# Token-major sums of squares ahead of the experts, and roots spread by a product of ones with a diagonal matrix

## The reference

```python
def rms_norm(x, g):
    xf = x.astype(F32)
    y = xf * lax.rsqrt(jnp.mean(xf * xf, axis=-1, keepdims=True) + EPS)
    return (y * g.astype(F32)).astype(x.dtype)

def modulate(x, g, shift, scale):
    return rms_norm(x, g) * (1.0 + scale) + shift
...
        x = x + g1 * m
        h = modulate(x, norm_ffn_g[l], sh2, sc2)
        x = x + g2 * hierarchical_moe(h, moe_w_group[l], moe_w_expert[l], moe_w_gate[l],
                                      moe_w_up[l], moe_w_down[l])
```

## Time and profile before

| | us |
|---|---|
| median of three runs | 918.23 |
| the three runs | 917.15, 918.23, 920.77 |
| the profiled execution | 921.55 |
| its span in the profile | 919.7 |

### The profile page before, as it was taken

The page is one execution under the profiler, slowest core; times in us unless marked ns, Lnnn a source line. Parts: engine busy times, 40 slices in busy tenths (PEclk is TensorE's granted clock), DMA queues, the critical chain, the costliest instruction groups (busy, mean ns, idle before and its releaser), DMA issues.

```text
span 919.7 us, 13173 instructions
## 1 busy us (share of the span) xinstructions
PE 762.9 (83%) x4683; PEld 428.4 (47%) x4683; DVE 359.8 (39%) x852; ACT 151.4 (16%) x358; POOL 176.0 (19%) x283
## 2 busy tenths in 40 slices
PE   1899977899988999877779876988899988778770
PEld 1544433468545655444445533736555544444430
DVE  0314427752353344333333333556234433333243
ACT  3112144630351110000000002443010000000000
POOL 0000210000003133322233220000233332323220
PEclk9999997999996999999999997995799999999995
DMA  9996630002876899999999997978399999999935
GB/s 351 428 407 278 239 61 0 12 1 109 355 292 222 345 409 416 422 420 421 420 421 423 390 424 291 425 320 306 124 400 390 417 423 424 421 422 422 421 123 205
DMA packets 39383, 294.33 MB, mean 320 GB/s; under 512 B 10584, under 2 KB 12048, under 8 KB 19376
## 3 DMA queue, kind: packets, MB, share of 16 engines
q1 hardware_dynamic: 26656, 275.49, 73.2%
q0 software_dynamic: 10880, 13.26, 4.7%
q10 hardware_dynamic: 1808, 5.06, 1.4%
HBM read 293.22 MB, written 22.02 MB: 343 GB/s over the span
## 4 chain that ended last, share of the span: by engine, by line
PE 60%; DMA 26%; DVE 6%; issue 3%; ACT 3%; SPq 1%; ACTq 0%; POOL 0%; POOLq 0%; DVEq 0%
DMA ring<-in_moe_w_in 19%; PE bank L1576 18%; PE bank L1600 8%; PE bank L1326 7%; PE bank L1257 4%; DMA adaw<-in_ada_w 3%; PE bank L1422 3%; PE bank L1552 3%; PE bank L1267 2%; DMA adaw<-results 2%; PE bank L1430 2%; PE bank L1383 2%; PE bank L1458 1%; PE bank L1439 1%; DMA rowsB<-in_ada_b 1%
## 5 line engine op out<-in xcount | busy, mean ns | idle before, releaser
L1576 PE MATMUL bank<-ring,qkv 128*64 128x256 f32 x2016 | 245.5, 398 | 59.6 <-issue 38.7
L1576 PEld LDWEIGHTS bank<-ring,qkv 128*64 128x64 f32 x2016 | 159.3, 143 | 128.0 <-issue 62.4
L1112 DVE COPY qkv<-bank 128x512 f32<-128x512 f32 x64 | 44.3, 692 | 222.6 <-PE bank L1552 222.6
L552 POOL DMA_INDIRECT results<-adaw,scur x65 | 67.0, 1031 | 310.0 <-DVE adaw L1135 260.4
L1600 PE MATMUL bank<-ring,qkv 128*64 128x512 f32 x504 | 122.0, 604 | 1.2 <-DVE qkv L1124 0.8
L809 ACT ACTIVATE qkv<-bank 128x128 f32<-128x128 f32 x64 | 17.7, 277 | 442.0 <-PE bank L1576 442.0
L542 POOL DMA_INDIRECT adaw<-rows,gcur x65 | 67.7, 1042 | 50.5 <-POOL gcur L539 50.5
L1326 PE MATMUL bank<-ring,hT 128*128 128x512 f32 x144 | 65.4, 609 | 1.2 <-DVE hT L874 1.2
L1600 PEld LDWEIGHTS bank<-ring,qkv 128*64 128x64 f32 x504 | 31.0, 136 | 47.5 <-issue 45.6
L1133 DVE SCALAR_TENSOR_TENSOR adaw<-qkv,wcur 128x512 f32<-128x512 f32 x64 | 48.1, 752 | 2.6 <-DVE wcur L1131 0.3
L1135 DVE SCALAR_TENSOR_TENSOR adaw<-bank,wcur,adaw 128x512 f32<-128x512 f32 x64 | 48.1, 751 | 2.3
(11 more groups left out here) (231 smaller groups left out, 765.2 us busy)
## 6 DMA issues: line engine op xcount, KB each, us to landing
ring<-in_moe_w_in SPq DMA_DIRECT2D x63, 2048.0 KB, 23.9
ring<-in_moe_w_out SPq DMA_DIRECT2D x63, 1024.0 KB, 20.5
adaw<-in_ada_w SPq DMA_DIRECT2D x13, 2048.0 KB, 13.0
ring<-in_ada_w SPq DMA_DIRECT2D x10, 2048.0 KB, 20.8
ring<-in_attn_w_qkv SPq DMA_DIRECT2D x3, 2048.0 KB, 36.1
ring<-in_attn_w_o SPq DMA_DIRECT2D x1, 4096.0 KB, 15.0
adaw<-in_moe_w_in SPq DMA_DIRECT2D x2, 2048.0 KB, 8.5
adaw<-results SPq DMA_DIRECT2D x8, 512.0 KB, 6.1
```

Source lines behind the costliest of these rows:

```text
L552: pool.indirect_dma_start(res, bass.IndirectOffsetOnAxis(ap=scur[:, p, :], axis=0), yout[:, p], None, bounds_check=res_limit, oob_is_err=F ...
L1112: V.tensor_copy(xgT[:, p], bank[2][:, :]).then_inc(xgT_ready, 1)
L1576: last = T.matmul(bank[p][64 * a:64 * a + 64, 0:2 * P], xk[:, k % 4, k // 4], w[:, :, k, a * P:(a + 1) * P], start=k == 0, stop=k == KD - ...
```

## The change

The sums become token-major: for each feature tile k and each of the three token tiles t, the squares are the stationary operand (128 features by 128 tokens) and a single column of ones moves, so that the sums of a token tile are one column of 128 partitions. The root and the reciprocal are then taken on 128x3. A diagonal matrix is made from each reciprocal column (128x384 in all), and one product of ones with it puts the reciprocal roots of all tokens on all partitions, in another part of the same PSUM bank, where VectorE reads them in lines 986 and 989. In TensorE's program this product, `root_rows`, stands between the sums and the ada products.

```diff
-        rstd = free[:, 3200 + 2 * NTOK:3200 + 3 * NTOK]
...
-                act.wait_ge(ms_ready, m + 1)
-                A.activation(rstd, rstd, ACT.Sqrt).then_inc(std_ready, 1)
+                act.wait_ge(st_mm, m * KD + KD)
+                A.activation(ss[:, 8:11], bank[STAT_BANKS[m]][:, 0:TT], ACT.Sqrt, scale=1.0 / D, bias=C("eps"))\
+                    .then_inc(std_ready, 1)
...
-                dve.wait_ge(st_mm, m * KD + KD)
-                V.tensor_scalar(rstd, bank[STAT_BANKS[m]][:, 0:NTOK], 1.0 / D, EPS, ALU.mult, ALU.add).then_inc(ms_ready, 1)
                 dve.wait_ge(std_ready, m + 1)
-                order(V.reciprocal(rstd, rstd))
+                order(V.reciprocal(ss[:, 12:15], ss[:, 8:11]))
+                V.tensor_tensor(dg[:, :, :], ident.unsqueeze(1).to_broadcast([P, TT, P]),
+                                ss[:, 12:15].unsqueeze(2).to_broadcast([P, TT, P]), ALU.mult).then_inc(root_ready, 1)
+                rstd = bank[STAT_BANKS[m]][:, P:P + NTOK]
+                dve.wait_ge(root_mm, m + 1)
...
             def norm_pe(n):
+                stat = bank[STAT_BANKS[n // 2]]
                 if n == 2:
                     pe.wait_ge(x_new[2], 8)
                 for k in range(KD):
                     pe.wait_ge(sq_ready, n // 2 * KD + k + 1)
-                    T.matmul(bank[STAT_BANKS[n // 2]][:, 0:NTOK], ones, sq[:, k % 2], start=k == 0, stop=k == KD - 1).then_inc(st_mm, 1)
+                    for t in range(TT):
+                        last = T.matmul(stat[:, t:t + 1], sq[:, k % 2, t * P:(t + 1) * P], ones[:, 0:1],
+                                        start=k == 0 and t == 0, stop=k == KD - 1, skip_group_check=True)
+                    last.then_inc(st_mm, 1)
+
+            def root_rows(n):
+                pe.wait_ge(root_ready, n // 2 + 1)
+                T.matmul(bank[STAT_BANKS[n // 2]][:, P:P + NTOK], ones, dg[:, :, :].rearrange("p t n -> p (t n)"),
+                         start=True, stop=True).then_inc(root_mm, 1)
 
             for l in range(2):
                 norm_pe(2 * l)
+                root_rows(2 * l)
```

More of the change, by code:

```diff
@@ L278, in build @@
         x_new = [sem(f"x_new{n}") for n in range(3)]
-        sq_ready, st_mm, ms_ready, std_ready, xr_ready, h_new, h_ctx = map(sem, (
-            "sq_ready", "st_mm", "ms_ready", "std_ready", "xr_ready", "h_new", "h_ctx"))
+        sq_ready, st_mm, root_ready, root_mm, std_ready, xr_ready, h_new, h_ctx = map(sem, (
+            "sq_ready", "st_mm", "root_ready", "root_mm", "std_ready", "xr_ready", "h_new", "h_ctx"))
         df_mm, df_even, df_odd, band_ready = map(sem, ("df_mm", "df_even", "df_odd", "band_ready"))
```

## The result

The changed kernel takes 924.08 us (median of 7 runs, 922.48 to 925.9), the kernel before, on the same chip, 917.71 (7 runs, 913.51 to 920.77). The ratio is 1.0071, with a 95% interval of 1.0047 to 1.0095: slower by 6.4 us, within 4.3 to 8.7. The prediction was 925.6, in a range of 918.5 to 930, 7.4 over the median it started from, and slower by over 0.5% with a chance of 0.67.

A forecast was written before the change was run, and what follows sets the result against it. Each norm was taken to count by how far it moves the router's product. Wait and lost clock together gave +5.0 to +10.3, middle +7.4, over the median of 918.23: 925.6 us, range 918.5 to 930.

The forecast's parts named there:

- What bounds it: Both norms: each is worth what it moves the router's product, passed on one to one through the experts' weight stream.
- The sums: Sums of each norm: six short passes take about 0.1 us less than a long looped step, gaining 0.3 in all.
- The roots: Behind the sums: root, reciprocal, diagonal and product of ones take 2.2 us, against about 3.8 before.
- the 0.3 for weights and drain: Product of ones behind the sums: some 0.3 us on top of its two passes of 0.32.
- The table load: Layer 0: ends 0.3 us behind the last sum, the root waits for it; no added drain of some 1.38.
- The operand in PSUM: Lines 986 and 989 reading one operand from PSUM: nothing added.
- The wait: Ada products behind the product of ones begin about 2.1 us after the sums: 0 in layer 0, +1.8 in layer 1.
- The clock: TensorE falls to 1.2 GHz during the sums or the wait behind them, both norms: +5.0 to +10.3 us, chance 0.75.
- the early one: Clock falls half-way through the sums: +4.0 us in layer 0, +6.3 in layer 1.
- the first experts run warm: Rival: first gate and up products and layer 1's router product meet the full clock, 6.1 us back, 914.0; chance 0.05.

The follow-up runs named there:

- wide_pass: The changed kernel with each short pass of the sums moving 128 columns of ones instead of one; ratio 1.0012 to the kernel before.
- layer0_alone: The change made in layer 0 only, layer 1 keeping the norm of the kernel before; ratio 1.0026 to the kernel before.

## Why the prediction was right

The direction and the mechanism held, a wait ahead of ada and a clock lost to narrow passes; several sizes did not, and part of the closeness of the number is luck. Point by point:

- *What bounds it.* Held from the first expert on. From its product in layer 0 to the sums of layer 1 the kernels take 301.5 and 301.3 (293.96 to 595.46; 294.00 to 595.29), and from the first expert of layer 1 to the end 271.1 and 270.6, so what reaches the first expert is passed on nearly whole. Between the router's product and the first expert it was not (last point).
- *The sums.* At the full clock two steps take 1.50 instead of 1.58, the 0.1 of the prediction; the 0.3 over all of them never came, as the clock was gone after the fifth step. For the steps at 1.2 GHz the text said three, of 1.4 each; three it was, of 1.2 each.
- *The roots.* Root 0.26, reciprocal 0.18, diagonal 0.56, product of ones 0.91 at the full clock: near the 2.2 of the text (0.29, 0.19, 0.56, 0.95 and hand-overs); the 0.3 for weights and drain, which had no row, came out as 0.27. The table load came out as said where the sums kept their clock. In wide_pass, where the sums end at 244.68, the root starts at 245.00, right as the load ends, with no drain in between. In the changed kernel the load is over at 243.60, ahead of the slower sums, and the root does not wait for it.

```profile
243.71 1.28 ACT L723 ACT_TABLE_LOAD   x1
245.00 0.26 ACT L723 ACTIVATE ss<-bank,con 128x3 f32<-128x3 f32 x1
```

- *The operand in PSUM.* 0.55 and 0.54 a product (lines 988 and 991), as from SBUF.
- *The wait.* Said 0 in layer 0 and +1.8 in layer 1; measured in wide_pass, with the clock kept, +0.3 and +2.3 (which hold 0.1 of slower sums each and, in layer 1, a little more of the stretch at 1.2 GHz that was there before).
- *The clock.* Said 5.0 to 10.3 for both layers with the wait, middle 7.4 (the middle of these two is in fact 7.65, and would have given 925.9). The fall was the early one, 3.4 to 4.0 us into the sums in all seven norms profiled with one-column passes: +3.7 and +6.0, 9.7 together, near that end's +4.0 and +6.3. Taking the middle mis-sized this term by 2.3.
- *What was missed.* Of these 9.7, the routers' stages gave back about 2 (36.85 to 36.2 in layer 0, 32.1 to 30.8 in layer 1, means of two profiles each), in layer 1 with fewer stretches at 1.2 GHz, in layer 0 for a reason that is open. The rival "the first experts run warm" held that such stretches can move with the time of arrival, though it placed them at the first experts and in the router's product. Two of these three stayed as they were (5.98 for the first expert's product of layer 0, 7.10 for the router's of layer 1); the first expert's product of layer 1 took 5.92 and 5.38 instead of 6.22 and 6.42, 0.7 less in the mean. The two misses, of 2.3 and of 2, offset each other by luck, so the forecast of +7.4 lies closer to +6.4 than its parts do. The 1.3 between 9.7 - 2 and 6.4 is that 0.7 in part, and the whole is within the measurement's interval.

Open is what exactly makes a router's stage keep or lose the clock from one execution to the next, and what else sets its length.

## What to carry to other kernels

- Making a product smaller is little gain when every pass needs a new weight load; passes of one column took 0.125 us at the full clock, passes of 128 took 0.13, and the narrow ones lost the full clock for the 10 us that followed. If few columns are needed, try feeding the wide operand anyway, when the bank has room.
- A short product that waits for other engines costs what stands behind it in TensorE's queue. Put it behind work that is ready, and first ask whether anyone waits for what it speeds up: in layer 1 nobody did.
- A change at the microsecond scale should be read by stage. Here the stages of one kernel repeated to 0.02 us, and a change of clock in them (22.11 instead of 20.86 in layer0_alone) was seen at once, while medians of the kernel before moved by 1.7 from one set of runs to another. But the stage behind must be read too: in layer 1 its length lay between 29.8 and 32.3 over the ten profiles.

## What was not expected of the hardware

A TensorE that issues passes without a gap can lose the full clock. In the changed kernel it is counted busy for 7.38 of 7.39 us of the sums, weight loads for 7.12, and the clock falls after five of eight steps (3.8 us into the sums in both layers). With 128 columns a pass it stays (1.00 in wide_pass), and stays over an idle 1.4 us too. Columns of work, not the count of instructions, made the difference in these runs. And one-column passes are a little quicker while the full clock lasts: 1.50 for two steps against 1.60 with 128 columns.
